# The down product takes its rows from 6 on first, with the low halves loaded back right behind the last up matmul

## The reference, cut to what matters

```python
u = rms_norm(x, lw['ln2_g']) @ lw['w_up']          # (t, 2 * 2816)
u_ext = jnp.concatenate([conv_prev.astype(u.dtype), u], axis=1)
c = lw['conv_b']
for i in range(CONV_W):                            # causal depthwise conv of 3 taps
    c = c + u_ext[:, i:i + t] * cw[i]
gate, val = jnp.split(c, [D_FF], axis=-1)
x = x + (jax.nn.silu(gate) * val) @ lw['w_down']   # (t, 2816) @ (2816, 1024)
```

## Time and profile before

| | us |
|---|---|
| median of 3 runs (lowest to highest) | 2534.99 (2529.2 to 2537.44) |
| the profiled execution, its own time | 2540.83 |
| its span, first to last instruction | 2538.7 |
| PE busy within the span | 2043.0 (80%) |
| DVE busy | 1158.4 (46%) |
| POOL busy | 593.6 (23%) |
| ACT busy | 510.0 (20%) |

### The profile page before, as it was taken

The page is one execution under the profiler, slowest core; times in us unless marked ns, Lnnn a source line. Parts: engine busy times, 40 slices in busy tenths (PEclk is TensorE's granted clock), DMA queues, the critical chain, the costliest instruction groups (busy, mean ns, idle before and its releaser), DMA issues.

```text
span 2538.7 us, 39805 instructions
## 1 busy us (share of the span) xinstructions
PE 2043.0 (80%) x16182; PEld 1958.6 (77%) x16182; DVE 1158.4 (46%) x1385; ACT 510.0 (20%) x992; POOL 593.6 (23%) x336
## 2 busy tenths in 40 slices
PE   0999979688888888268237776795999999968998
PEld 0999979677777777257236676794999999968998
DVE  6564023066656776125333335626665666630000
ACT  3232101033322223021222331202212122110000
POOL 1222223322212221020001111231233333313332
PEclk9999989889999999678556568997999999989999
DMA  3622422211110112510132112330222212243221
GB/s 126 160 72 75 92 68 93 89 33 53 53 31 24 53 53 107 216 47 23 44 138 84 47 60 92 118 132 31 75 70 72 67 67 75 71 183 116 87 86 58
DMA packets 108114, 205.79 MB, mean 81 GB/s; under 512 B 34896, under 2 KB 71936, under 8 KB 107264
## 3 DMA queue, kind: packets, MB, share of 16 engines
q10 hardware_dynamic: 85472, 111.21, 13.6%
q1 hardware_dynamic: 22544, 93.09, 11.1%
HBM read 151.72 MB, written 71.37 MB: 88 GB/s over the span
## 4 chain that ended last, share of the span: by engine, by line
PE 69%; DVE 12%; issue 8%; DMA 5%; ACT 3%; ACTq 2%; POOL 1%; SPq 0%; DVEq 0%; POOLq 0%
PE bank L1543 39%; PE bank L1912 9%; PE bank L1591 3%; PE bank L1844 2%; PE bank L1829 2%; PE bank L1694 2%; PE bank L1699 1%; PE bank L1864 1%; DMA hlo<-hloT 1%; PE bank L1627 1%; DVE ydev L1125 1%; PE bank L1837 1%; PE bank L1686 1%; DVE tt L1189 1%; PE bank L1561 1%
## 5 line engine op out<-in xcount | busy, mean ns | idle before, releaser
L1543 PE MATMUL bank<-ahi,whi 128*128 128x344 f32 x2256 | 744.7, 330 | 73.8 <-DVE alo L1471 24.3
L1543 PE MATMUL bank<-ahi,wlo 128*128 128x344 f32 x2256 | 726.3, 322 | 0.0
L1543 PE MATMUL bank<-alo,whi 128*128 128x344 f32 x2256 | 726.2, 322 | 0.0
L417 POOL TENSOR_SCALAR whi<-wraw 128x1024 fp32r<-128x1024 f32 x130 | 143.4, 1103 | 1569.0 <-PE bank L1543 1184.6
L1543 PEld LDWEIGHTS bank<-ahi,whi 128*128 128x128 f32 x2256 | 429.6, 190 | 85.1 <-issue 37.6
L1543 PEld LDWEIGHTS bank<-alo,whi 128*128 128x128 f32 x2256 | 429.0, 190 | 6.9 <-issue 4.4
L1543 PEld LDWEIGHTS bank<-ahi,wlo 128*128 128x128 f32 x2256 | 429.0, 190 | 0.0
L419 POOL TENSOR_TENSOR wlo<-wraw,whi 128x1024 fp32r<-128x1024 f32 x130 | 341.8, 2629 | 10.9
L1912 PE MATMUL bank<-hhi,whi 128*128 128x344 f32 x528 | 172.2, 326 | 27.1 <-DMA hlo<-hloT 27.1
L1912 PE MATMUL bank<-hlo,whi 128*128 128x344 f32 x528 | 171.4, 325 | 0.0
L1912 PE MATMUL bank<-hhi,wlo 128*128 128x344 f32 x528 | 171.4, 325 | 0.0
(11 more groups left out here) (305 smaller groups left out, 2973.3 us busy)
## 6 DMA issues: line engine op xcount, KB each, us to landing
wraw<-in_wst SPq DMA_DIRECT2D x130, 512.0 KB, 3.6
hloT<-hlo_st ACTq DMA_DIRECT2D x22, 516.0 KB, 2.7
gT<-stage ACTq DMA_DIRECT2D x16, 516.0 KB, 2.7
stage<-gT ACTq DMA_DIRECT2D x16, 516.0 KB, 3.3
rwT<-stage ACTq DMA_DIRECT2D x14, 516.0 KB, 2.9
pin<-rwT ACTq DMA_DIRECT2D x8, 903.0 KB, 7.0
out_qkT<-stage ACTq DMA_DIRECT2D x12, 516.0 KB, 2.7
hlo<-hloT ACTq DMA_DIRECT2D x1, 5676.0 KB, 31.8
```

What stands on the lines that cost most here:

```text
L417: nc.gpsimd.tensor_scalar(whi[:, s], wraw[:, s], 1.0, 0.0, ALU.mult, ALU.add).then_inc(sem("w_hi"), 1)
L1543: last = pe.matmul(out[:, 0:PC], wpart[a][:, s, k], apart[b][:, k, n * PC:(n + 1) * PC], start=(k == 0 and (a, b) == (0, 0)), stop=(k == K ...
```

## The change

The order of the rows in the down product becomes `DN_ORDER`: 6 to 20, then 0 to 5, then 21. The blocks of the down weights are laid out in that order on the host, so that tile n still holds its blocks in the order of use. The four loads become rows 6 and 7, rows 8 to 11, rows 12 to 20, and rows 0 to 5. The first three lie over `ahi` and `alo` alone; ACT issues them directly behind the up loop, once the last up matmul is done and rows 0 to 20 are stored. Row 21 is not stored and loaded at all: DVE subtracts it straight into its place in `hlo` (`last_low_part`). When that is done, ACT issues the fourth load. PE begins the down product when row 20's high half is there, and in tile 0 it makes the two passes with `hhi` of all eight rows (48 matmuls) before the pass with `hlo` (24 matmuls). In the other tiles the passes stand per row as before, with the order of the second and third exchanged. DVE also waits for the fourth load ahead of its first `yst`, which lies over `hlo`'s neighbours.

```diff
-HLO_PARTS = ((0, 1), (1, 4), (4, 11), (11, KF))
+DN_ORDER = tuple(range(6, KF - 1)) + tuple(range(6)) + (KF - 1,)
+HLO_PARTS = ((6, 8), (8, 12), (12, KF - 1), (0, 6))
...
+            def load_low(n):
+                a, b = HLO_PARTS[n]
+                act.dma_start(hlo[:, a:b].bitcast(F32), hloT[a:b].rearrange("c p t -> p c t"))\
+                    .then_inc(sem(f"hlo_loaded{n}"), 16)
+
             peeled(act, KF, up_pair)
+            act.wait_ge(sem("hlo_stored"), 16 * (KF - 1))
+            act.wait_ge(sem("mm_piece"), P_DN)
+            for n in range(3):
+                load_low(n)
             high_part(KF - 1)
-            store_low_part(KF - 1)
-            act.wait_ge(sem("hlo_stored"), 16 * KF)
-            act.wait_ge(sem("mm_piece"), P_DN)
+            act.wait_ge(sem("h_lo"), KF)
             for s in range(2):
                 act.wait_ge(sem(f"row_stored{s}"), 16 * KF)
-            for n, (a, b) in enumerate(HLO_PARTS):
-                act.dma_start(hlo[:, a:b].bitcast(F32), hloT[a:b].rearrange("c p t -> p c t"))\
-                    .then_inc(sem(f"hlo_loaded{n}"), 16)
+            load_low(3)
...
+            def last_low_part():
+                dve.wait_ge(sem("h_hi"), KF)
+                dve.wait_ge(sem("mm_piece"), P_DN)
+                TT_(hlo[:, KF - 1], cc[:, 1], hhi[:, KF - 1].bitcast(F32), ALU.subtract).then_inc(sem("h_lo"), 1)
...
-            low_part(KF - 1)
+            last_low_part()
+            dve.wait_ge(sem("hlo_loaded3"), 16)
...
-            pe.wait_ge(sem("h_hi"), KF)
+            pe.wait_ge(sem("h_hi"), KF - 1)
...
+            def down(o, n, at, k, passes):
+                for c in range(3):
+                    for a, b in passes:
+                        last = pe.matmul(bank[3 * (o % 2) + c][:, 0:PC], wpart[a][:, n % 2, at % 8],
+                                         hpart[b][:, k, c * PC:(c + 1) * PC],
+                                         start=(at == 0 and (a, b) == (0, 0)),
+                                         stop=(at == KF - 1 and b == 1))
+                return last
...
+                    if n == 0:
+                        for at in range(8):
+                            down(o, n, at, DN_ORDER[at], ((0, 0), (1, 0)))
+                    for at in range(8 * j, min(8 * j + 8, KF)):
+                        k = DN_ORDER[at]
+                        if o == 0:
+                            for m_, (a_, _) in enumerate(HLO_PARTS):
+                                if k == a_:
+                                    pe.wait_ge(sem(f"hlo_loaded{m_}"), 16)
+                            if k == KF - 1:
+                                pe.wait_ge(sem("h_lo"), KF)
+                        last = down(o, n, at, k, ((0, 1),) if n == 0 else ((0, 0), (1, 0), (0, 1)))
                     last.then_inc(sem("mm_down"), 1)
```

More of the change, by code:

```diff
@@ L1943, in lay_out @@
     dn = blocks(a["w_down"][0])
-    dn = np.concatenate([dn, np.zeros((KD, P, 24 - KF, P), f)], 2).reshape(KD, P, 3, 8, P)\
+    dn = np.concatenate([dn[:, :, list(DN_ORDER)], np.zeros((KD, P, 24 - KF, P), f)], 2).reshape(KD, P, 3, 8, P)\
         .transpose(0, 2, 1, 3, 4).reshape(3 * KD, P, 8, P)
```

## The result

The changed kernel takes 2511.73 us in the median of 7 runs (2505.67 to 2515.43), the kernel before 2528.86 in 7 runs (2521.73 to 2537.44, the three runs shown above among them). The ratio is 0.9928, with a 95% interval of 0.9906 to 0.9950: faster by 17 us, or by 13 to 24 us over the interval. The forecast was 17.2 us less.

The account below looks back on a forecast made before the run. Bound: landing of the last blocking load, plus matmuls left, plus clock cost. 2272.6 + 1518 x 0.1577 + 3.0 = 2515.0 against 2532.2, 17.2 us less; 2534.99 - 17.2 = 2517.8, predicted 2518, range 2511 to 2525.

Parts of the forecast that it names:

- D: Distance from the last up matmul's end to the last down matmul's end; 283.6 us before, 266.4 expected after.
- the base of the absolute time: Median of the runs of the kernel before, 2534.99 us, from which the gain of 17.2 us was subtracted.
- the exchange of passes: Down product: swapping the second and third pass costs nothing, since matmuls start 0.16 us apart whichever pass follows.
- Leaving the loops: End of the up loop, ahead of the early loads: nearly 0 us for loading code, bounds 0 and 2.6 us.
- The loads: Early low-half loads between up and down stage: about 1.28 us a row, landing at 2254.7, 2261.1 and 2272.6.
- The clock: TensorE in the down product: lower clock after the 9.6 us wait for the third load, costing 3.0 us.
- The matmuls' time: Down product after the third load: 1518 matmuls at 0.1577 us, plus 3.0 us for the clock.
- The cover of the fourth load: Down product, row 0: load lands at 2280.3, TensorE wants it at 2286.5, 6 us of cover.
- The best bound: Seam's best case: earlier issue, 1.26 us a row, 2.7 us of clock: 2.2 us better; without clock fall, gain at most 22.
- Late loads: Rival: early loads go out only when the last low half is ready, 2259.4; gain 9 us, time 2526; chance 0.08.
- Hidden gain: Rival: in the down product TensorE gets ahead and later waits for weights; time about 2535; chance 0.04.
- slower clock: Rival: bursts and gaps starting the down product keep the clock at its lower level long after; time 2543; chance 0.03.

Follow-up runs that it names:

- the kernel with late loads: Changed kernel, but its three early loads issued only behind the last low half, with the fourth: 2519.24 us median, 0.9954 of before; D 272.5 us.
- gaps filled: Changed kernel plus 20 and 44 matmuls with unused results ahead of the waits for the second and third load: D 267.3 us.
- two and three tiles first: Changed kernel, high-half passes of tiles 0 and 1 made first: 2507.22 us; on that kernel, tile 2's too, ahead of the wait for rows 1 to 5: 2502.57 us.
- row 21 direct alone: Kernel before, with only the last row's low half subtracted straight into place, neither stored nor loaded: D 277.3 us, against 283.6 before.

## Why the prediction was right in its mechanism, and the step of it that failed

**The mechanism and the gain were right.** 17.2 us were forecast, 17.1 is the difference of the medians, 18.4 that of D. That the first two agree to a tenth is partly luck: the interval runs from 13 to 24 us, and in D a late load and faster matmuls, below, partly cancel.

**The step that failed** is the base of the absolute time: "the forecast for a median is 2534.99 - 17.2 = 2517.8". The median of three runs stood 6.1 us above that of seven, and the result came out 6.3 us under 2518. Put on the median of 7 runs, 2528.86, the same 17.2 us give 2511.7. A range for an absolute time had to hold the spread of its base, 8.2 us in the three runs shown, and 2 us at either end were too little: the result lies only 0.7 us inside it. Within the gain the term that failed is one put at nothing, "the exchange of passes costs nothing": it is worth 0.9 us.

**Term by term**, behind the last up matmul's end:

| | predicted | measured |
|---|---|---|
| first down matmul | 0.6 | 0.7 |
| 48 matmuls done | 8.2 | 8.4 |
| loads begin to be issued | 1.2 | 1.3 |
| first, second, third load landed | 6.1, 12.5, 24.0 | 7.0, 13.4, 24.9 |
| matmuls left then | 1518 | 1518 |
| their time | 242.4 | 240.3 |
| D | 266.4 | 265.2 |

- *Leaving the loops* costs nothing, as taken: ACT's first load is issued 0.23 us after the last transfer of the loop, TensorE starts 0.24 us after ACT has emptied the bank. Both bounds of code loading (up to 2.6 us) were too wide here.
- *The loads* came 0.9 us late, nearly all of it with the first: two rows took 5.7 us instead of 4.9 (5.1 in the kernel with late loads, where the weight tile was out of the way). From there on the rate of 1.28 us a row and the price of the weight tile were right. That was partly luck. The prediction read 1.28 from the first three loads of before and passed over the fourth, whose eleven rows took 16.8 us (2278.5 to 2295.3), 1.53 each, with a packet of instructions at 2285 and a weight tile from 2288.5 on among them; and where such a packet fell into the early loads, they ended about 1.5 us later (gaps filled, two and three tiles first). The Trainium skill, DMA: Bandwidth & Descriptors (Specifications), gives about 358 GB/s from HBM for a core; the trace disagrees here too, with 411 to 416 GB/s.
- *The clock.* I expected the fall behind the second gap only. It fell in the first, of 3.98 us, and cost the 12 matmuls there, hidden by the wait that followed; behind the third load 25 matmuls took 6.0 us, 2.1 us extra where I had taken 3.0. The Trainium skill, TensorE: Matmul & The Clock Gate (Part 1), says that the engine falls to half the clock when it idles and gets it back by working; the rows agree, 0.50 behind the gaps and 1.00 in the stream.
- *The matmuls' time* was put 2.1 us too high. 0.7 us of it is the price of 0.1577 us, too high for the old order itself: 220 us of the stream of before hold 1399 matmuls, 0.1573 us each. 0.9 us is *the exchange of passes*, priced at nothing: the 1518 matmuls take 241.1 us with the old order and 240.3 with the new. The prediction took the equal 0.16 us in the rows, a rounded figure, for equality. The rest, some 0.5 us, is left for the clock.
- *The cover of the fourth load* held: no wait stands between the third load and the end of the stage.
- *The best bound* doesn't come out of its own terms: 0.1 us of issue, 0.3 of rate over 16 rows and 0.3 of clock are 0.7 us, not 2.2, so the mechanism's own range began at about 2514 and not at 2513.

**The rivals.** Late loads: in a kernel made so, 7.2 us are given back where 8.3 were counted. So these 7.2 us hang on ACT's place, and not "the whole gain", as the prediction had it: 11.1 us are left with late loads, where it had counted 9. Hidden gain and slower clock: neither shows; from 2263.4 on TensorE is busy 234.27 of 234.30 us at clock 1.00.

## What to carry to other kernels

Where a stage waits for several loads in one queue, its end is the landing of the last load that has no cover plus the work left at that moment; starting the consumer earlier counts only by the work that it gets done before that landing (6.3 us of earlier start were worth 1.7). Move the issue of the loads to the moment when their destination comes free, let the part that can't be loaded yet come last, and put work that needs none of the loads in front; then ask again which load is waited for, since the cover of the next one is used up. Read such an edit by a distance inside the program, not by the span, when stages ahead of it vary by 15 us from execution to execution.

## What the runs showed of the hardware that I had not expected

- The order of the three passes changes the rate of the down matmuls by 0.4% (1405 or 1406 against 1399 in 220 us of unbroken stream, in every kernel of either order that has such a stretch) and that of the up matmuls not at all (1261 in 198 us with either). The cause is open.
- The length of a gap alone does not tell whether the clock falls. Gaps of 3.71 and 3.98 us brought the lower clock while TensorE still idled, and the gap of 2.43 us before did not bring it. But gaps of 2.76 and 2.38 us in the kernel with row 21 direct alone did, 1.5 and 1.3 us after the matmuls had resumed, at 0.51 for 3.5 and 3.3 us. The prediction's "6.66 us brought it and 2.43 us did not" is no rule.
- A packet of instructions within the early loads goes with a last one that lands about 1.5 us later (four kernels with it, five without). The cause is not shown.
- The same attention code ran 183.5 us in one execution and 174.3 in another, at a mean granted clock of 0.61 and 0.70.
